# Loading the experts' weight matrices with consecutive rows in one partition (one core, two layers with 64 experts)

## The reference, cut to what matters

```
h = _modulate(_rms(x, norm_g[l, 2]), sh_f, sc_f)         # (256, 1024)
scores = sigmoid(h @ router_w)                           # 64 experts, 8 are taken per token
gates  = normalised scores of the chosen experts, else 0
def _swiglu(t, w_gu, w_dn):                              # w_gu (1024, 512), w_dn (256, 1024)
    gate, up = split(t @ w_gu, 2)
    return (silu(gate) * up) @ w_dn
moe = _swiglu(h, sh_gu, sh_down) + sum_e gates[:, e] * _swiglu(h, exp_gu[e], exp_down[e])
x = x + g_f * _rms(moe, norm_g[l, 3])
```

## Time and profile before

| what | value |
|---|---|
| time, median of 3 runs | 1989.82 us (1989.31 to 1991.47) |
| profiled execution, first to last instruction (its span) | 1988.7 us |
| what of the median lies outside such a span | 1.1 us |
| PE busy | 1851.3 us, 93% |
| DVE busy | 586.6 us, 29% |
| DMA queue of SP | 530.35 MB in 227440 packets |
| HBM read over the span | 543.69 MB |

### The profile page before, as it was taken

One profiled execution on the slowest core, in us unless ns is written; L12 is line 12 of the kernel. 1 busy time (PEld: TensorE's weight loads), 2 busy tenths in 40 slices (PEclk: granted clock), 3 DMA queues, 4 the chain that ended last, 5 costly groups with the idle time before them and its releaser, 6 DMA issues.

```text
span 1988.7 us, 27315 instructions
## 1 busy us (share of the span) xinstructions
PE 1851.3 (93%) x11186; PEld 974.7 (49%) x11186; DVE 586.6 (29%) x1555; ACT 298.0 (15%) x609; POOL 56.2 (3%) x74
## 2 busy tenths in 40 slices
PE   5999986789999999999989999879999999999986
PEld 4876553344444444444434886444444444444432
DVE  3302357353222222222224337442222222222212
ACT  2210133112111111111102000011111111111101
POOL 0100010030000000000000000010000000000000
PEclk8999998889999999999999999999999999999998
DMA  9776580466999999999965230456999999999763
GB/s 368 265 268 260 189 298 1 167 229 246 359 357 352 356 354 358 358 349 358 334 240 215 85 127 0 147 209 253 351 353 360 353 356 350 358 356 355 291 239 148
DMA packets 231907, 545.54 MB, mean 274 GB/s; under 512 B 7456, under 2 KB 7664, under 8 KB 230960
## 3 DMA queue, kind: packets, MB, share of 16 engines
q1 hardware_dynamic: 227440, 530.35, 72.9%
q0 software_dynamic: 3376, 14.40, 2.0%
q10 hardware_dynamic: 1040, 0.07, 0.0%
HBM read 543.69 MB, written 1.09 MB: 274 GB/s over the span
## 4 chain that ended last, share of the span: by engine, by line
PE 85%; DVE 7%; DMA 4%; ACT 2%; issue 1%; SPq 1%; DVEq 0%; PEldq 0%
PE bank L530 81%; DMA gu<-in_exp_gu 2%; PE bank L855 1%; DMA gu<-in_w_mod 1%; DMA gu<-in_w_in_ab 1%; ACT zone L958 1%; PE bank L830 1%; DVE zone L1337 1%; PE bank L563 1%; DVE zone L1320 1%; DVE hh L1214 0%; ACT hh L958 0%; DVE x L1217 0%; DVE hh L1431 0%; SPq L383 0%
## 5 line engine op out<-in xcount | busy, mean ns | idle before, releaser
L530 PE MATMUL bank<-gu,zone 128*64 128x512 f32 (+1 forms) x2272 | 523.2, 601 | 21.6 <-DMA gu<-in_exp_gu 16.4
L530 PE MATMUL bank<-zone 128*128 128x128 bf16 (+1 forms) x3976 | 479.4, 277 | 17.2 <-DVE zone L1437 8.9
L530 PEld LDWEIGHTS bank<-zone 128*128 128x128 bf16 (+1 forms) x3976 | 305.1, 113 | 228.2 <-issue 218.2
L958 ACT ACTIVATE zone<-bank 128x256 f32<-128x256 f32 (+1 forms) x389 | 176.9, 473 | 1250.4 <-PE bank L530 679.3
L530 PEld LDWEIGHTS bank<-gu,zone 128*64 128x64 f32 (+1 forms) x2272 | 167.6, 140 | 327.7 <-issue 322.5
L530 PE MATMUL bank<-dn,zone 128*64 128x512 f32 (+2 forms) x1312 | 313.9, 575 | 12.9 <-ACT zone L958 12.9
L1537 DVE COPY zone<-bank 128x512 f32<-128x512 f32 x138 | 95.5, 692 | 334.7 <-PE bank L530 334.7
L530 PEld LDWEIGHTS bank<-dn,zone 128*64 128x64 f32 (+1 forms) x1312 | 106.6, 150 | 154.6 <-issue 129.7
L1532 DVE TENSOR_TENSOR zone<-zone,bank 128x256 f32<-128x256 f32 x69 | 29.1, 421 | 403.7 <-ACT zone L958 403.7
L530 PE MATMUL bank<-hl,gu 128*128 128x256 f32 x640 | 140.1, 380 | 0.7 <-ACT hl L958 0.7
L530 PEld LDWEIGHTS bank<-hl,gu 128*128 128x128 f32 x640 | 121.7, 190 | 17.3 <-ACT hl L958 1.0
(11 more groups left out here) (224 smaller groups left out, 947.0 us busy)
## 6 DMA issues: line engine op xcount, KB each, us to landing
gu<-in_exp_gu SPq DMA_DIRECT2D x138, 2048.0 KB, 11.1
dn<-in_exp_down SPq DMA_DIRECT2D x138, 1024.0 KB, 12.4
gu<-in_w_mod SPq DMA_DIRECT2D x24, 2048.0 KB, 12.0
gu<-in_w_in_ab SPq DMA_DIRECT2D x7, 2048.0 KB, 18.1
gu<-in_w_in_hy SPq DMA_DIRECT2D x6, 2048.0 KB, 10.4
gu<-in_w_out_ab SPq DMA_DIRECT2D x2, 2048.0 KB, 9.2
gu<-in_sh_gu SPq DMA_DIRECT2D x2, 2048.0 KB, 9.1
gu<-in_w_out_hy SPq DMA_DIRECT2D x2, 2048.0 KB, 7.8
```

The lines of the kernel that those rows point to most:

```text
L530: return pe.matmul(o, lhsT, rhs, start=start, stop=stop, skip_group_check=True)
L958: return nc.scalar.activation(o, i, f, **kw)
```

## The change

The experts' up and down matrices, the shared expert's two and the router's matrix are loaded with consecutive rows in one partition: partition `p` gets rows `8p` to `8p+7` of an up matrix, one stretch of 16 KB, and rows `2p` and `2p+1` of a down matrix, 8 KB. For the router it is 2 KB. Bytes, slots, semaphores and the order of the transfers stay.

The feature sides follow. In the norm ahead of each MoE (`i` is 2 or 4) the SCALAR_TENSOR_TENSOR walks `x` and the scale in order and writes feature `8q+k` to column `128k+q` of `hh`, so each written element lies 512 bytes from the one before it; the addition walks `hh` in order and reads the shift table with a step of 32 bytes. Column blocks, transposes, bf16 parts and gathers of `hh` then need no change. The hidden values are turned by even and odd columns (a step of 8 bytes) in place of first and second half. The norms ahead of the mixers and all other weights stay. No instruction is added, removed or moved on any engine.

```
-  src = a["sh_gu"][l].rearrange("(k p) n -> p k n", p=P) if kind == "sh" else src[kind][:, :, cols]
+  src = a["sh_gu"][l].rearrange("(p k) n -> p k n", p=P) if kind == "sh" else src[kind][:, :, cols]
-  sp.dma_start(dn[:, 3], a["sh_down"][l].rearrange("(f p) n -> p f n", p=P)).then_inc(dn_in, 16)
+  sp.dma_start(dn[:, 3], a["sh_down"][l].rearrange("(p f) n -> p f n", p=P)).then_inc(dn_in, 16)
-  sp.dma_start(gu[:, j], a["exp_gu"][l][bass.ds(e, 1)].rearrange("a (k p) n -> p (a k) n", p=P)).then_inc(
+  sp.dma_start(gu[:, j], a["exp_gu"][l][bass.ds(e, 1)].rearrange("a (p k) n -> p (a k) n", p=P)).then_inc(
-  sp.dma_start(dn[:, j], a["exp_down"][l][bass.ds(e, 1)].rearrange("a (f p) n -> p (a f) n", p=P)).then_inc(
+  sp.dma_start(dn[:, j], a["exp_down"][l][bass.ds(e, 1)].rearrange("a (p f) n -> p (a f) n", p=P)).then_inc(
-  pool.dma_start(rw, a["router_w"][l].rearrange("(k p) e -> p k e", p=P)).then_inc(r_in, 16)
+  pool.dma_start(rw, a["router_w"][l].rearrange("(p k) e -> p k e", p=P)).then_inc(r_in, 16)
-  last = pe.transpose(bank[:, 7, f * P:(f + 1) * P], sg2[:, t, f * P:(f + 1) * P], ident)
+  last = pe.transpose(bank[:, 7, f * P:(f + 1) * P], sg2[:, t, f:F:2], ident)
-  last = pe.transpose(bank[:, 7, f * P:(f + 1) * P], he[:, f * P:(f + 1) * P], ident)
+  last = pe.transpose(bank[:, 7, f * P:(f + 1) * P], he[:, f:F:2], ident)
   step(v.reciprocal(st[:, s + 3:s + 4], st[:, s + 2:s + 3]))
+  if i in (2, 4):
+      step(v.scalar_tensor_tensor(hh[:, t, :].rearrange("p (k q) -> p q k", k=KT), src.rearrange("p (q k) -> p q k", k=KT),
+                                  st[:, s + 3:s + 4], table[:, m + 1, :].rearrange("p (q k) -> p q k", k=KT), ALU.mult, ALU.mult))
+      turned = hh[:, t, :].rearrange("p (k q) -> p k q", k=KT)
+      v.tensor_tensor(turned, turned, table[:, m, :].rearrange("p (q k) -> p k q", k=KT), ALU.add).then_inc(nrm_h, 1)
+      return
```

## The result

| | before | after |
|---|---|---|
| median of 20 runs each, taken together | 1990.12 us (1988.69 to 1992.54) | 1993.79 us (1991.31 to 1996.81) |
| ratio, 95% interval | | 1.0017 [1.001, 1.0023] |
| span of the profiled execution | 1988.7 us | 1992.0 us |

The account below looks back on a forecast made before the run. PE was taken to set the pace, waiting only at three loads of up matrices. Gains of 7.1 us there less 2.5 us for the norms gave -4.6 us, 1985.2 us against 1989.8, range 1973 to 1999.

Parts of the forecast that it names:

- the hidden values' transposes at nothing: In the pair loops, the transposes' step of 8 bytes was taken as 0, with bounds 0 and 18 us.
- a pair's time that moves: Sign of being wrong in the pair loops: a pair was to stay at 17.69 us.
- rows 9: Profile rows cited for the transposes: line 809's 64 columns with a 16-byte step and line 530's contiguous loads, both 137 ns.
- forecast 2.5: Cost of the four norms ahead of the MoEs: 0.7 us each, less 0.3 hidden in layer 0; upper bound 13.7 us.
- Rival 3: The four changed norms cost their upper bound, 13.7 us, giving +6.6 us, about 1996 us; chance 0.12.
- 3.6 us each: PE's three waits for up matrices before further pairs, each 1.9 us shorter through faster loads, 5.7 us together.
- 400 GB/s from the second on: Sign in the waited-for up loads: single microseconds behind their issue reach 400 GB/s from the second on.
- the 1.4 forecast: Gain in up matmuls behind the three waits: the smallest of three clock penalties, 1.4 us, taken back.
- the 2.9 us of the text: Time after PE stopped at which the granted clock fell; the 3.6 us wait left was still longer.
- The pair loops' cover: PE's 17.69 us a pair hide the weight loads, so faster loads gain nothing there.
- Rival 4: Long pieces lower the sustained rate in the pair loops: at 340 GB/s 45 us more, about 2034 us; chance 0.10.
- rival 2: Slow start comes from two 2 MB loads at once, not layout: gain 0, cost 2.5, about 1992 us; chance 0.16.

Follow-up runs that it names:

- turns_only: Kernel before with only the hidden values' transposes read by even and odd columns, loads unchanged, so MoE sums differ: 1994.65 us in one run.
- turns_64: Down matrices and their stepped transposes alone changed from before, with each pair's second transpose cut to 64 of 128 columns: 1969.52 us, one further pair fewer.
- loads_only: Kernel before with only the experts' and shared expert's loads in the new layout, so MoE sums differ: 2002.34 us in one run, one further pair more.
- up_plain: Up matrices, router and norms changed against before, but the norms' SCALAR_TENSOR_TENSOR in plain order and only the addition writing with a step: 1988.32 us, ratio 0.9986.
- up_pool: Up matrices, router and norms as in the change, against before, with POOL's split of the first token tile waiting for the second norm: 1991.84 us, ratio 1.0002.
- the up side alone: Up matrices, router and norms as in the change, down matrices and hidden values' transposes as before: 1989.32 us against 1990.17, ratio 0.9996.
- up_plain_pool: Up matrices, router and norms changed against before, SCALAR_TENSOR_TENSOR plain, only the addition's writes stepped, POOL's first-tile split waiting for the second norm: 1987.02 us, ratio 0.9981.

## Why the prediction was wrong, point by point

**The failed step: the hidden values' transposes at nothing.** The two stretches that hold the pairs became 4.9 us longer. The step alone makes them 4.2 us longer (`turns_only`), and either figure turns the forecast's -4.6 into about no change. The text had named a pair's time that moves as a sign of being wrong, and it moved, from 17.69 to 17.76 us. The term itself was in the text: 128 columns in each of the two loads, with a bound of 18 us, and I discarded it by rows 9. That row was the wrong witness twice. It has 64 columns, and in the pair's second load 64 columns take 160 ns with the step and 128 take 218 (`turns_64`, `turns_only`). And I compared a transpose with a matmul's load, two kinds with other times: in the same trace before, a transpose's contiguous 128 columns take 142 ns and a matmul's (line 530, weights from `gu`) 190. A step at the same kind and the same width was nowhere in the trace, so the term belonged in the sum at an estimate between the bounds, not at zero. The mechanism is shown from both sides by `turns_only` and `loads_only`.

The Trainium skill, "SBUF — State Buffer", in its note on cachelines, says that two hits in a 16-byte line are enough for full rate. By it a float32 step of 8 bytes, with two elements in each line, is free. The rows on line 855 say 214 ns for 142, and the measurement decides.

**Norms: right place, undersized.** This is the second failed term: forecast 2.5, measured 6.8 us. Of the price of a step, 0.7 ns an element, the addition's part was right (2.00 for 1.225 us is 0.76 ns an element). The scattered write was taken as 0 and costs the same: 1.974 for 1.285 us, 0.67 ns an element, shown by `up_plain`. Against what the text said, the number of elements staying the same was no reason. The timelines show how the rest divides. The eight instructions of the four norms are 7.0 us longer in all than before. The steps are 5.9 us of it (four times 0.69 and 0.78), and of these the scattered writes, left out of the sum, 2.8. Contention with POOL's split is the other 1.1: it puts 2.6 and 2.0 us on the second norms of the two layers (0.9 and 1.7 us on the two instructions in layer 0, gone in `up_pool`), but before it put 1.0 and 2.5 us there too.

The same norms cost 5.5 us from norm to pair in the up side alone, with instructions as long, so some 1.3 of the 6.8 us is not theirs. The clock is the likely place, which no run separates. The 16 matmuls of the shared expert behind the norms took 9.99 and 9.65 us in layer 0, before 8.80 and 7.09, and in the up side alone 9.53 and 7.08. Ahead of the first of these blocks the longer idle time of PE (4.01 us) is a reason: the granted clock was 0.80 in the microsecond from 394 and 0.50 from 395 on. Why it fell once more, to 0.54 in the microsecond from 415, and gave the 9.65 stays open. Rival 3 had the place but not the size, 13.7 us.

The Trainium skill, "SBUF — State Buffer", on the port pair that DVE and GpSimd (POOL) share, says that one of them blocks while the other holds it, where a DVE instruction with two SBUF inputs meets one of GpSimd's that reads SBUF. The timelines of `up_plain` agree within 0.2 us. POOL's subtraction (line 487) starts at 403.78, while DVE's plain instruction runs until 404.78. With the 2.12 us that it takes in `up_pool`, counted from there, it would end at 406.90; it ends at 406.77. The addition starts at 404.82, and with its 1.94 us of `up_plain_pool` counted from POOL's end it would end at 408.71; it ends at 408.53.

**The waits: right, with rates that were not.** 3.6 us each were forecast, 3.59, 3.72 and 3.44 came. The time from issue to PE's start fell from 14.69 to 12.94 us, where the forecast has 12.8. But I had taken 421 GB/s from 1.3 us after the issue on, which makes 330 over the first six microseconds. It is 300, with 229 and 213 in the second and third microsecond, so the sign "400 GB/s from the second on" failed. In the rest it is 425, where before has 239 and 390:

```profile
1923.66:1929.66 6.00, 6.00 (x44) 3.12 (x45) 1.27 (x2) 1.47 (x3) 0.00 (x0) 1.00 0.83 300
1929.66:1936.60 6.94, 3.22 (x10) 1.27 (x9) 1.68 (x8) 0.38 (x1) 0.00 (x0) 1.00 1.00 425
```

The slower start costs some 0.4 us (0.18 MB at 421 GB/s). The higher rate behind it and 4.75 MB in place of 4.8 give some 0.2 back, so the wait came out better than its parts. By the Trainium skill, "DMA: Bandwidth & Descriptors", section "Why small descriptors are slow (HBM only)", the estimate was 4% for longer packets. In the second stretches it is 9% here, 6% in the up side alone.

**The clock behind the waits: not a term that can be counted on.** It gave 2.2 us back here for the 1.4 forecast, and took 1.5 us more in the up side alone at nearly the same waits. The length of the wait does not decide it. Behind 3.44 us the next block took 7.09 us here and 9.89 in `up_plain`; behind 3.59 us it took 7.09 in `loads_only` and 8.78 here. Nor are the 2.9 us of the text a fixed time: in the change's second wait, of 3.72 us, the granted clock was still 1.00 when PE began again at 1936.60, and 0.89 and 0.50 in the two microseconds from 1936.66. So the 2.2 us are luck of this execution as far as these traces show.

**The pair loops' cover held**, as forecast: no waits for weights, 354 GB/s, fewer busy DMA engines. Rival 4 is refuted (its 2034 us also leaves out the -4.6 of the rest of the sum), and so is rival 2, since the load did become faster with the layout.

**The range.** The measured 1993.8 us lies inside 1973 to 1999, though outside the forecast's own 1980.5 to 1989.5, between rivals 2 and 3. That is luck: neither rival's mechanism alone put it there, and half of what did was a term that the text had at nothing.

**A version that beats both** follows: take the fast loads where they are waited for, leave the down side alone, and pay the norm's step once. `up_plain` is at 0.9986 [0.9975, 0.9996] of before, and with POOL held back at 0.9981 [0.9972, 0.999], some 3 to 4 us faster. The change as it stands is at 1.0017.

## What to carry to other kernels

A layout that helps a transfer moves its price to whoever reads or writes the other side, so count those instructions first: here the down matrices were never waited for, and their half of the change could only lose. A small fee that the trace before can't show (56 ns in one weight load) decides when it stands on PE's own chain 69 times; a row with another width or another kind of operation does not prove it zero. And before an engine is held back to spare another one contention, look at what it will run beside instead.

## What the runs showed that I had not expected

- A float32 step in DVE costs 0.67 to 0.76 ns an element at 1024 elements, whether it is the output's (512 bytes) or an input's (32 bytes), and one instruction with an output step and plain inputs costs no more (1.90 for 1.225 us).
- PE's weight load of 128 float32 columns for a transpose takes 142 ns in plain order and 214 with a step of 8 bytes; 64 columns take 160 with that step (means 218 and 160 in the same place).
- How long the idle time before a block is does not tell what the clock takes from it: behind 3.44 us, 32 matmuls took 7.09 us in one execution and 9.89 in another.
- Loads in pieces of 16 KB keep the DMA engines busy for 0.88 of the time at 354 GB/s, in 2 KB pieces for 0.97 at 355, which was worth nothing to this kernel.
